# The order of work where one weight sweep of a float32 backbone kernel ends and the next begins

## The reference, cut to what matters

```python
for i in range(DEPTH):                                   # DEPTH = 2
    m = jnp.split((sc @ w_mod[i] + b_mod[i])[:, None, :], N_MOD, axis=-1)
    h = h + 0.5 * m[2] * _swiglu(_modulate(_rmsnorm(h, ffn1_norm[i]), m[0], m[1]), ffn1_w1[i], ffn1_w3[i], ffn1_w2[i])
    n_lat = _modulate(_rmsnorm(h, mix_norm[i]), m[3], m[4])
    y, yc = _token_mixing(n_lat, n_ctx, w_in[i], w_out[i], ...)   # pooling | latent attention | differential attention
    h = h + m[5] * y
    h = h + 0.5 * m[8] * _swiglu(_modulate(_rmsnorm(h, ffn2_norm[i]), m[6], m[7]), ffn2_w1[i], ffn2_w3[i], ffn2_w2[i])
    # the same for the context stream, with mc in the place of m; after layer 0 only the latents go on
return _rmsnorm(h, final_norm)
```

## Time and profile before

| | |
|---|---|
| time, median of 3 runs | 3028.47 us (3025.4 to 3030.12) |
| the profiled execution | 3029.08 us, its span in the trace 3027.1 us |
| PE busy | 2908.7 us, 96% of the span |
| DVE busy | 1662.7 us, 55% |
| ACT busy | 889.0 us, 29% |
| mean share of the 16 DMA engines that q1 takes | 28.2% |
| mean granted clock of PE | 0.984 of full |

### The profile page before, as it was taken

The page is one execution under the profiler, slowest core; times in us unless marked ns, Lnnn a source line. Parts: engine busy times, 40 slices in busy tenths (PEclk is TensorE's granted clock), DMA queues, the critical chain, the costliest instruction groups (busy, mean ns, idle before and its releaser), DMA issues.

```text
span 3027.1 us, 43891 instructions
## 1 busy us (share of the span) xinstructions
PE 2908.7 (96%) x16914; PEld 2486.0 (82%) x16914; DVE 1662.7 (55%) x3086; ACT 889.0 (29%) x1389; POOL 104.9 (3%) x82
## 2 busy tenths in 40 slices
PE   7999999999989989999999999999999989899998
PEld 3888888888856768888888888888888757798996
DVE  4776578643366557865777435433343466443343
ACT  4221122232346432211222322122233255322222
POOL 0000000025000000000000000000014000000000
PEclk9999999999999989999999999999999999999999
DMA  5334243322300024342443123212223300233232
GB/s 197 122 121 130 86 132 120 108 68 64 86 1 1 22 70 132 120 123 91 132 126 97 57 62 104 82 58 62 74 59 75 79 1 1 70 90 104 83 95 72
DMA packets 422725, 255.37 MB, mean 84 GB/s; under 512 B 25985, under 2 KB 418025, under 8 KB 422634
## 3 DMA queue, kind: packets, MB, share of 16 engines
q1 hardware_dynamic: 422634, 254.13, 28.2%
HBM read 252.01 MB, written 2.10 MB: 84 GB/s over the span
## 4 chain that ended last, share of the span: by engine, by line
PE 92%; DVE 3%; ACT 3%; issue 1%; DMA 0%; SPq 0%; DVEq 0%; ACTq 0%
PE pair L725 56%; PE pair L721 25%; PE pair L900 2%; PE pair L852 2%; PE pair L640 2%; PE pair L868 1%; PE pair L590 1%; PE pair L877 1%; DVE lo_w L1273 1%; PE pair L828 1%; ACT buf L1153 1%; PE pair L885 1%; PE pair L810 1%; DVE mod_acc L1428 1%; ACT hi_w L970 1%
## 5 line engine op out<-in xcount | busy, mean ns | idle before, releaser
L725 PE MATMUL pair<-n_hi,hi_w 128*128 128x258 f32 (+2 forms) x3456 | 855.7, 329 | 38.9 <-DVE lo_w L1273 24.9
L725 PE MATMUL pair<-n_lo,hi_w 128*128 128x258 f32 (+2 forms) x3456 | 851.9, 328 | 0.0
L725 PE MATMUL pair<-n_hi,lo_w 128*128 128x258 f32 (+2 forms) x3456 | 851.3, 327 | 0.0
L725 PEld LDWEIGHTS pair<-n_hi,hi_w 128*128 128x128 f32 x3456 | 542.8, 192 | 99.8 <-issue 33.9
L725 PEld LDWEIGHTS pair<-n_lo,hi_w 128*128 128x128 f32 x3456 | 542.5, 192 | 57.1
L725 PEld LDWEIGHTS pair<-n_hi,lo_w 128*128 128x128 f32 x3456 | 542.0, 192 | 57.0
L1273 DVE TENSOR_TENSOR lo_w<-raw_w,hi_w 128x1024 fp32r<-128x1024 f32 (+1 forms) x296 | 396.7, 1340 | 319.2 <-ACT hi_w L970 318.6
L970 ACT CAST hi_w<-raw_w 128x1024 fp32r<-128x1024 f32 (+1 forms) x296 | 328.1, 1110 | 646.5 <-PE pair L725 358.0
L1428 DVE SCALAR_TENSOR_TENSOR mod_acc<-mod_w,silu_c,mod_acc 128x256 f32<-128x256 f32 x896 | 364.6, 478 | 0.0
L721 PE MATMUL pair<-h_hi,hi_w 128*128 128x512 f32 x1232 | 340.3, 346 | 6.4 <-DVE lo_w L1273 6.4
L1351 DVE TENSOR_TENSOR buf<-pair,rstd 128x512 f32<-128x512 f32 (+1 forms) x308 | 164.7, 570 | 327.8 <-PE pair L725 327.8
(11 more groups left out here) (182 smaller groups left out, 2027.3 us busy)
## 6 DMA issues: line engine op xcount, KB each, us to landing
raw_w<-in_ffn_w SPq DMA_DIRECT2D x176, 512.0 KB, 3.8
mod_w<-in_w_mod SPq DMA_DIRECT2D x64, 1024.0 KB, 5.1
raw_w<-in_ffn_w SPq DMA_DIRECT2D x64, 704.0 KB, 4.7
raw_w<-in_w_in SPq DMA_DIRECT2D x38, 512.0 KB, 3.9
pro_w<-in_w_mod SPq DMA_DIRECT2D x2, 4096.0 KB, 18.0
raw_w<-in_w_out SPq DMA_DIRECT2D x16, 512.0 KB, 4.1
x_tok<-in_x SPq DMA_DIRECT2D x4, 512.0 KB, 5.2
out<-x_tok SPq DMA_DIRECT2D x4, 512.0 KB, 2.6
```

Source lines behind the costliest of these rows:

```text
L725: mm = pe.matmul(pair[s][:, a:a + m], wt[:, k * P:(k + 1) * P], src[:, of(k):of(k) + m], start=opens, stop=closes)
```

## The change

The numbers of instructions of PE and DVE stay as they are, apart from branches; only places move. Line numbers shift by up to 49.

1. **Modulation batch ahead of the fold.** In FFN sweeps without a paired first unit, the first batch stands right behind slot 1's lo_w, ahead of `mod_evict`; in the paired ones it stands at the end of `norm_x`, ahead of the wait for rstd. Its partial sums go to the other of the two buffers mod_part.
2. **Second slot behind the first.** In the paired first units slot 1 runs LAG = 4 rows behind slot 0 (`first_pair`); the norm's sums stand between row 4 of slot 0 and row 0 of slot 1. `out_pair` has slot 1 one or two rows behind.
3. **Weights split sooner.** In paired sweeps ACT makes unit 1's hi_w of slot 0 ahead of the first silu or square. Between `out` and ffn2_up ACT makes n_hi for k = 0 and 1 first, then hi_w of slot 1, then the last square, then the other six k; DVE makes n_lo for k = 0 and 1 ahead of slot 1's lo_w.

```diff
+LAG = 4
+def pairs_up(w):
+    return starts_norm(w) and late_rows(w) or w["what"] == "out"
...
+            def first_pair(w, sums):
+                open_slot(w, 0, 0, True)
+                for n in range(KD + LAG):
+                    if n < KD:
+                        norm_row(n)
+                        row(w, n, 0)
+                    if n == LAG:
+                        if sums:
+                            sum_stream(sums)
+                        open_slot(w, 0, 1, True)
+                    if n >= LAG:
+                        row(w, n - LAG, 1)
+
+            def out_pair(w):
...
+                row(w, 0, 0)
+                values_mla(L, last)
+                pe.wait_ge(out_dve, L * N_DVE + 2)
+                row(w, 1, 0)
+                open_slot(w, 0, 1, True)
+                row(w, 0, 1)
+                row(w, 1, 1)
...
+                for h in range(1, HEADS):
+                    turn_diff(L, h, n)
+                    pe.wait_ge(mix_ready, L * HEADS + h)
+                    row(w, M_DIFF + h - 1, 0)
+                    row(w, 2 + h, 1)
+                pe.wait_ge(mix_ready, L * HEADS + HEADS)
+                row(w, KD - 1, 0)
+                for k in range(KD - 2, KD):
+                    row(w, k, 1)
...
             def norm_x(w_cols, w):
                 if w is not None:
-                    split_hi(w, 0, 1, True)
                     if late_rows(w) and w["base"]:
...
-                            act.wait_ge(pair_free[s], before["base"] + before["n"])
                         shift_high(w)
-                        for k in range(KD):
+                        high(0, w_cols)
+                        high(1, w_cols)
+                        split_hi(w, 0, 1, True)
+                        finish(before, before["n"] - 1, 1)
+                        act.wait_ge(pair_free[0], before["base"] + before["n"])
+                        for k in range(2, KD):
                             high(k, w_cols)
...
+                if pairs_up(w):
+                    split_hi(w, 1, 0, False)
                 finish(w, 0, 0)
...
+                if late_rows(w):
+                    shift_low(w)
+                    low(0, w_cols)
+                    low(1, w_cols)
                 split_lo(w, 0, 1)
                 if late_rows(w):
-                    shift_low(w)
-                    for k in range(KD):
+                    for k in range(2, KD):
                         low(k, w_cols)
                     cnt["n"] += KD
+                    if mod_tile(w) is not None:
+                        mod_add(w, 0, 0, KD)
                 wait_rstd()
...
-                if q and mod_tile(SWEEPS[q - 1]) is not None:
+                folds = q and mod_tile(SWEEPS[q - 1]) is not None
+                if per and not pairs_up(w):
+                    mod_add(w, 0, 0, KD, 1 if folds else 0)
+                if folds:
                     mod_evict(SWEEPS[q - 1])
...
-                if per:
-                    mod_add(w, 0, 0, KD)
                 finish(w, 0, 0)
```

More of the change, by code:

```diff
@@ L692, in turn_diff, with row @@
                 mm.then_inc(turned_diff, 1)
-            def unit(w, i, slots, first, sums=0):
+            def row(w, k, s):
                 down = w["what"].endswith("_down")
                 src_hi, src_lo = (h_hi, h_lo) if down else (n_hi, n_lo)
[L698 to L703, removed]
-                for k in range(w["kt"]):
[L705 to L726, removed]
-                        if k == w["kt"] - 1:
-                            mm.then_inc(unit_done[s], 1)
-                    if sums and k == 4:
-                        sum_stream(sums)
@@ new lines, in row @@
+                hi, lo = hi_w[s], lo_w[s]
+                for wt, src in ((hi, src_hi), (hi, src_lo), (lo, src_hi)):
+                    opens, closes = k == 0 and wt is hi and src is src_hi, k == w["kt"] - 1 and wt is lo
+                    if down or w["what"] == "out":
+                        for a, m in halves(width(w, s)):
+                            mm = pe.matmul(pair[s][:, a:a + m], wt[:, k * P:(k + 1) * P], tile(src, k, m, a),
+                                           start=opens, stop=closes)
+                    else:
+                        for a, m, of in streams(w, s):
+                            mm = pe.matmul(pair[s][:, a:a + m], wt[:, k * P:(k + 1) * P],
+                                           src[:, of(k):of(k) + m], start=opens, stop=closes)
@@ new lines, in row, with open_slot, norm_row, unit @@
+                if k == w["kt"] - 1:
+                    mm.then_inc(unit_done[s], 1)
+            def open_slot(w, i, s, first):
+                pe.wait_ge(lo_ready[s], w["base"] + i + 1)
+                if not (first and w["base"] == 0):
+                    pe.wait_ge(pair_free[s], w["base"] + i)
+            def norm_row(k):
+                if k == 0:
+                    pe.wait_ge(shift_ready, cnt["n"] // KD + 1)
+                pe.wait_ge(n_ready, cnt["n"] + k + 1)
+            def unit(w, i, s, first):
+                open_slot(w, i, s, first)
+                for k in range(w["kt"]):
+                    if first and s == 0:
+                        if w["what"].endswith("_down"):
+                            pe.wait_ge(h_ready, cnt["h"] + k + 1)
+                        else:
+                            norm_row(k)
+                    row(w, k, s)
@@ L1079, in sweep @@
                     shift_high(w["to"])
+                if pairs_up(w):
+                    split_hi(w, 1, 0, False)
                 finish(w, 0, 0)
                 def between(i):
-                    split_hi(w, i, 0, False)
+                    if not (pairs_up(w) and i == 1):
+                        split_hi(w, i, 0, False)
                     if w["what"] == "in" and w["arg"] == 12 and i == 1:
@@ L1092, in between @@
                     finish(w, i, 0)
-                if ends_step(w) or w["what"] == "in" and w["arg"] == 12:
+                if ends_step(w) or pairs_up(w) or w["what"] == "in" and w["arg"] == 12:
                     for i in range(1, w["n"]):
@@ L1101, in sweep @@
                     split_hi(SWEEPS[q + 1], 0, 0, True)
-                finish(w, w["n"] - 1, 1)
+                if w["what"] != "out":
+                    finish(w, w["n"] - 1, 1)
                 if ends_step(w) and w["to"] is not None and not late_rows(w["to"]):
```

70 lines of the change are left out of this document (33 added, 37 removed).

## The result

The changed kernel takes 2976.31 us (median of 4 runs, 2972.47 to 2978.58); the kernel before, run beside it, 3027.56 us (4 runs, 3025.4 to 3030.12). The ratio is 0.983, with a 95% interval of 0.9814 to 0.9845. The profiled execution took 2978.58 us, its span is 2976.8 us, its mean granted clock 0.990; before they were 3029.08, 3027.1 and 0.984.

The account below looks back on a forecast made before the run. PE bounds the kernel (92% of the chain that ended last), so only its waits and slow clock can be won. Terms 18.2 + 13.4 + 8.2 + 4.4 + 5.2 + 1.9 = 51.3 us off 3029.08 give 2977.8; range 2969 to 2994 (0.88).

Parts of the forecast that it names:

- Batch, four edges: Second up and down sweeps of ffn1 and ffn2: lo_w waits and clock go; 4.4, 4.9, 4.4, 4.5 us, together 18.2.
- The sum: Whole kernel: all gains add to 51.3 us, 34.7 of it waits and 16.6 clock.
- ffn2_up of layer 0: Earlier start, pair ending at 1117.7, no wait behind it: 10.8 us plus 2.6 of clock, 13.4 us.
- ffn2_up of layer 1: The same in 512 columns without a batch: pair ends 5.5 us sooner plus 2.7 of clock, 8.2 us.
- First pair: Kernel's first sweep: 3.6 us and 2.6 of clock, less a new 1.8 us wait for slot 1 of unit 1; net 4.4.
- `out`: The two `out` pairs: waits shrink to 0.8 and 1.2 us; gains 5.2 us in layer 0, 1.9 in layer 1.
- Rival A: Waits go, but 1.2 GHz stretches come elsewhere and return about 10 us: 2988 us; chance 0.16.
- Rival B: Paired rows run at 1.2 GHz behind the norm's sums, losing 25 us: 3003 us; chance 0.04.
- Rival C: Slabs land late, so slot 1 of unit 1 waits 4 to 5 us longer in paired sweeps: 2987 us; chance 0.06.
- Rival D: Only the moved batch takes effect, pairs' ends being set by something unlisted: 3011 us; chance 0.04.
- Rival E: Slower: DVE stands at moved batches whose mod_w hasn't landed; 3048 us at 10 us each; chance 0.02.
- Mean clock: Whole kernel: mean granted clock rises from 0.984 to about 0.995, a sign the prediction is right.

Follow-up runs that it names:

- rows alone: Kernel before with only PE's row order moved (slot 1 four rows behind slot 0, `out` pairs with slot 0 ahead); 3010.81 us, ratio 0.9946.
- the kernel cut at four k: Changed kernel with the loop's modulation batch cut after four of its eight k instead of six (MOD_CUT = 4); 2977.82 us, ratio 0.9837.
- rows and weights: Kernel before with PE's new row order and ACT's and DVE's earlier weight splits, modulation batch not moved; 3000.85 us, ratio 0.9906.
- batch and rows: Kernel before with the modulation batch moved and PE's new row order, without ACT's and DVE's earlier weight splits; 2986.48 us, ratio 0.9866.
- batch alone: Kernel before with only the modulation batch moved ahead, in paired and other sweeps; 3005.79 us, ratio 0.993.

## Why the prediction was right, point by point

- *Batch, four edges.* 4.4, 4.9, 4.4, 4.5 predicted; 4.7, 5.2, 4.7, 4.9 measured, and the same to 0.02 us in every kernel that moves the batch. The waits were exact, and each edge gave 1.8 us beside its wait where 1.5 of clock were booked. The clock was booked rightly. The kernel with the rows alone has the wait of the second ffn1_up without the slow stretch behind it (1.00 over the 6 us; the last section shows the window):

```profile
365.18 0.62 PE L690 MATMUL pair<-n_hi,hi_w 128*128 128x512 f32 x2 [2.90 <-DVE lo_w L1307]
```

  There the sweep is 1.51 us shorter than before, which is the clock, and 3.17 us longer than in the changed kernel. The last 0.27 us go with the wait itself: the profile counts idle time from the modelled end of the last matmul, and PE loses 3.07 us from start to start there and 0.10 more at the next matmul. The sum had no term for that. The slack of 3.0 us is 3.5, the 2.0 at the down sweeps 2.8.
- *ffn2_up of layer 0.* 13.4 predicted, 14.1 measured: 2.8 off the pause (5.76 to 2.95) and 11.3 in the sweep. The credit that the sum gave to single steps (the early start, the earlier row 4, the batch beside the n_lo chain) is borne out by the kernels without each of them: 11.0 and no pause gained without the weights, 5.3 and the pause gained without the batch.
- *ffn2_up of layer 1.* 8.2 predicted; 2.5 + 6.0 = 8.5 measured.
- *First pair.* 4.4 predicted, 5.0 measured. The new wait came where it was said (93.59, forecast near 92) and is 1.09 us instead of 1.8; the kernel cut at four k shows that the loop's batch ahead of the readout makes it. But the prediction laid it to the change as a whole, and it comes with the third part: with rows and weights, the batch not moved, PE waits 1.32 us there; with the rows, or batch and rows, it doesn't, and waits 0.8 us for slot 0 of that unit instead. The first sweep by itself is 5.8 us shorter than before in those two kernels, 5.1 with rows and weights and 5.0 in the changed one, so here the early weights cost some 0.7 us.
- *`out`.* 5.2 and 1.9 predicted, 5.6 and 1.8 measured; 0.46 and 1.13 us of wait stay, where 0.8 and 1.2 were booked.
- *The sum.* The edges give 54.5 us for 51.3 forecast, each but one a little more. Against that stand 4.5 us in the `in` sweeps and mixers of both layers, which the change doesn't touch; with 0.4 in the tail, 50.3 of the span. The two errors offset each other, and that the total came out so close is in part luck. Rival A, the clock that returns elsewhere, would describe the 4.5 us, at about half its price of 10; that the change brings them isn't shown. Over the traced kernels these two stretches lie between 0.5 us below and 1.9 above before, and between 0.0 and 3.9 above, wherever ACT's order in them is the old one, and in the kernel with batch and rows nothing came back. The sum has no term for this clock.
- *Rival B, the pairs at 1.2 GHz.* Layer 0's ffn2_up pair, begun at 1075.72 and joined by slot 1 behind the sums, runs at full clock from 1082 us on:

```profile
1082.00:1085.00 3.00, 3.00 (x14) 1.00 0.02 5
1085.00:1088.00 3.00, 3.00 (x17) 1.00 0.01 3
1088.00:1094.00 6.00, 6.00 (x37) 1.00 0.14 33
```

  The slots alternate row by row from 1085.67 to about 1093. The Trainium skill, *TensorE: Matmul & The Clock Gate*, section *A second HAM failure mode: psum-queue depth-cycling*, tells of a kernel that cycles through PSUM banks, idles shortly between its groups of matmuls and has its clock swing by it. These rows show no swing; and where the page speaks of a swing, rival B had priced a clock that stays low.
- *Rival C, late second slots.* In the sweeps that the change touches no second slot made PE wait but that at 93.59. *Rival D, only the batch:* the batch alone gives 19.2 us. *Rival E:* at 349.29 DVE goes from lo_w straight into the moved batch, its slab being there.
- *Mean clock, 0.995 forecast, 0.990 measured: wrong, and by the prediction's own numbers.* At 0.984 about 2 x 0.016 x 3027 = 97 us run at 1.2 GHz; 16.6 us of clock at 45% are 37 us of it, 60 are left, and 1 - 60 / (2 x 2977) = 0.990. The figure was guessed beside the sum instead of taken from it.

## What to carry to other kernels

Where a vector engine works in order, look for work that needs nothing and stands ahead of a readout that the matmul engine will need: moved into the idle time before, it is free up to its slack, and the slack can be read off and tried by padding it. When two slots run interleaved, let the first end ahead of the pair by as much as readout and weight split take (here 2.4 us, two to three rows), and count the rows that follow its last. Parts of such a change can need each other: the early n_hi gained 0.4 us alone and 2.8 with the rows that no longer ask for the second slot at the start.

## What the runs showed of the hardware

The same wait at the same place lowers the clock in one kernel's profiled execution and not in another's. Behind the 2.90 us wait of the second ffn1_up, in the kernels with rows alone and with rows and weights:

```profile
365.18:371.18 6.00, 6.00 (x34) 1.00 0.31 90
```

```profile
366.12:372.12 6.00, 6.00 (x25) 0.72 0.32 90
```

In the first the edge is 1.5 us shorter than before, with the wait as it was. Layer 1's `out` does the opposite: behind its 3.08 us wait the clock stayed at 1.00 before, and in the kernel with the batch alone the same 3.08 us are followed by

```profile
2554.19:2560.19 6.00, 6.00 (x19) 0.72 0.48 140
```

and the stretch is 1.5 us longer. The prediction took the 1.00 there to be a property of the place; it isn't. What decides it was not settled: the waits agree to 0.02 us, and only the time at which the stretch comes differs. In size the clock costs about 1.5 us at each such wait, and over layer 1's `in` and mixer, where PE's program never changed, up to 3.9 us. The spread from run to run goes with it too: the changed kernel took 2973.76 us at a mean clock of 0.993 and 2978.91 at 0.990. A gain of 1 us from a wait removed can't be seen in such times; in the stretches of the trace it can.
